# A two-FFN decoder layer on one core: block sums of the Strassen weights moved to GpSimd, with new orders on ScalarE, VectorE and TensorE

## The reference

```python
def _half_ffn(x, norm_g, w_gate, w_up, w_down):
    h = _rmsnorm(x, norm_g)
    return x + 0.5 * ((jax.nn.silu(h @ w_gate) * (h @ w_up)) @ w_down)
# reference(), for the prompt and for the samples
xp = _half_ffn(xp, ffn1_norm, ffn1_w_gate, ffn1_w_up, ffn1_w_down)
u, q, k, v = _project(_rmsnorm(xp, mix_norm), pos_p, w_in, q_norm, k_norm)
mixed = concat([_pool_mix(u, ...), _swa_prompt(q, k, v, attn_sinks)], -1)
xp = xp + mixed @ w_out
xp = _half_ffn(xp, ffn2_norm, ffn2_w_gate, ffn2_w_up, ffn2_w_down)
```

## Time and profile before

| | |
|---|---|
| Median of 3 runs | 915.8 us |
| Lowest to highest | 915.64 to 920.76 us |
| The profiled execution's own time | 918.1 us |
| Its span in the trace | 916.3 us |
| TensorE clock granted, mean | 0.992 of full |
| PE, DVE, ACT, POOL busy | 95%, 75%, 48%, 10% of the span |

### The profile page before, as it was taken

One profiled execution on the slowest core, in us unless ns is written; L12 is line 12 of the kernel. 1 busy time (PEld: TensorE's weight loads), 2 busy tenths in 40 slices (PEclk: granted clock), 3 DMA queues, 4 the chain that ended last, 5 costly groups with the idle time before them and its releaser, 6 DMA issues.

```text
span 916.3 us, 17091 instructions
## 1 busy us (share of the span) xinstructions
PE 867.6 (95%) x6943; PEld 848.0 (93%) x6943; DVE 689.3 (75%) x1046; ACT 436.2 (48%) x702; POOL 89.1 (10%) x84
## 2 busy tenths in 40 slices
PE   9999989998999997999999999998899979999888
PEld 8998989998999997999889999998899979999888
DVE  7976788887888864755885887857888778887744
ACT  8632355545545542434753575423554455554410
POOL 0000011111111100013332001000111111111000
PEclk9999999999999998999999999999999999999989
DMA  8122666686757731422301517227665867677221
GB/s 306 48 82 69 199 158 145 148 199 180 169 122 189 194 83 56 177 84 79 124 25 60 170 61 204 63 70 222 159 152 125 221 171 156 133 197 194 70 93 70
DMA packets 62799, 124.27 MB, mean 136 GB/s; under 512 B 5345, under 2 KB 20833, under 8 KB 62721
## 3 DMA queue, kind: packets, MB, share of 16 engines
q1 hardware_dynamic: 48208, 98.16, 33.6%
q0 software_dynamic: 12784, 22.55, 16.3%
q10 hardware_dynamic: 1728, 2.48, 0.7%
HBM read 119.22 MB, written 3.60 MB: 134 GB/s over the span
## 4 chain that ended last, share of the span: by engine, by line
PE 73%; DVE 14%; issue 5%; DMA 4%; ACT 3%; SPq 1%; DVEq 0%; ACTq 0%
PE ps L757 16%; PE ps L878 14%; PE ps L880 14%; PE ps L879 14%; PE ps L960 10%; DMA full<-gu 4%; DVE wlo L1806 4%; DVE hlo L1927 3%; PE ps L1129 1%; PE ps L1111 1%; ACT whi L1363 1%; DVE hfull L1913 1%; PE ps L1120 1%; DVE gate L1862 1%; ACT u2c L1379 1%
## 5 line engine op out<-in xcount | busy, mean ns | idle before, releaser
L878 PE MATMUL ps<-xhi,whi 128*128 128x260 f32 (+1 forms) x1092 | 313.9, 287 | 35.8 <-ACT u2c L1379 23.2
L879 PE MATMUL ps<-xlo,whi 128*128 128x260 f32 (+1 forms) x1092 | 310.9, 285 | 0.0
L880 PE MATMUL ps<-xhi,wlo 128*128 128x260 f32 (+1 forms) x1092 | 310.5, 284 | 0.0
L878 PEld LDWEIGHTS ps<-xhi,whi 128*128 128x128 f32 x1092 | 205.9, 189 | 41.9 <-issue 28.8
L1806 DVE TENSOR_TENSOR wlo<-full,whi 128x1024 fp32r<-128x1024 f32 (+1 forms) x165 | 210.8, 1305 | 0.0
L880 PEld LDWEIGHTS ps<-xhi,wlo 128*128 128x128 f32 x1092 | 206.5, 189 | 0.0
L879 PEld LDWEIGHTS ps<-xlo,whi 128*128 128x128 f32 x1092 | 206.3, 189 | 0.0
L879 PE MATMUL ps<-hlo,whi 128*128 128x268 f32 (+1 forms) x336 | 95.5, 284 | 0.0
L880 PE MATMUL ps<-hhi,wlo 128*128 128x268 f32 (+1 forms) x336 | 95.4, 284 | 0.0
L878 PE MATMUL ps<-hhi,whi 128*128 128x268 f32 (+1 forms) x336 | 95.4, 284 | 0.0
L2398 POOL DMA_DIRECT2D full<-gu x31 | 37.4, 1207 | 455.2 <-DMA full<-gu 455.2
(11 more groups left out here) (220 smaller groups left out, 1522.8 us busy)
## 6 DMA issues: line engine op xcount, KB each, us to landing
full<-gu SPq DMA_DIRECT2D x78, 512.0 KB, 4.7
full<-gu POOLq DMA_DIRECT2D x31, 512.0 KB, 6.1
full<-d SPq DMA_DIRECT2D x32, 384.0 KB, 3.7
full<-gu SPq DMA_DIRECT2D x39, 256.0 KB, 4.5
full<-d POOLq DMA_DIRECT2D x16, 384.0 KB, 5.3
full<-d SPq DMA_DIRECT2D x8, 768.0 KB, 4.2
raw<-w_in SPq DMA_DIRECT2D x10, 512.0 KB, 3.8
raw<-gu SPq DMA_DIRECT2D x8, 512.0 KB, 3.9
```

The lines of the kernel that those rows point to most:

```text
L878: nc.tensor.matmul(dst, whi_t, mhi_t, start=(first and pr == 0), stop=False, skip_group_check=True)
L879: nc.tensor.matmul(dst, whi_t, mlo_t, start=False, stop=False, skip_group_check=True)
L880: last = nc.tensor.matmul(dst, wlo_t, mhi_t, start=False, stop=(pr == pairs - 1), skip_group_check=True)
```

## The change

1. **Sums.** GpSimd issues no adding transfers any more. It makes all four sums of every Strassen unit itself, 39 x 4 of 128x512 and 16 x 4 of 128x384, in the order block 1 (`s3_made`), 2 (`s2_made`), 5 (`s4_made`), 4 (`s1_made`). VectorE makes none.
2. **Orders.** ScalarE and VectorE cast and split a whole unit ahead: in unit v stand `hi_a`, `hi_b`, `hi_c` of v+1 on ScalarE, with `silu_0` last, and `lo_c` of v, `lo_a` and `lo_b` of v+1 on VectorE. `make_std` moves from the second unit to the first, `pair_sums` ahead of `take_single`, and in whole units the splits go ahead of the other work.
3. **TensorE.** P2 goes ahead of P5. P3 of the last gate unit comes behind two k tiles of the down product, P4 behind three, and in part 3 the last k tiles of the first two output tiles come behind the others of both.
4. **Loads.** Transfer a no longer waits for P2 of the unit three earlier; whole loads and casts wait for P6 instead of P4.

```diff
-                names = [("P1", v), ("P7", v), ("P3", v - 1), ("P6", v), ("P4", v - 1), ("P5", v), ("P2", v)]
+                names = [("P1", v), ("P7", v), ("P3", v - 1), ("P6", v), ("P4", v - 1), ("P2", v), ("P5", v)]
...
             sp.dma_start(full[:, r, 1:5:3, 0:w], src[:, 2:3, :].to_broadcast([P, 2, w])).then_inc(c_loaded[r], 16)
-            if strassen(s, v - 3):
-                sp.wait_ge(products, product_no(s, v - 3, "P2"))
             sp.dma_start(full[:, r, 0:4:3, 0:w], src[:, 0:2, :]).then_inc(a_loaded[r], 16)
...
                     if q == 0:
-                        down(s, v, 0, [0])
+                        down(s, v, 0, [0, 1])
                         p3(s, v - 1)
+                        down(s, v, 0, [2])
                         p4(s, v - 1)
-                        down(s, v, 0, list(range(1, t)))
+                        if unit[1] == 3:
+                            down(s, v, 0, list(range(3, t - 1)))
+                            down(s, v, 1, list(range(t - 1)))
+                            down(s, v, 0, [t - 1])
+                            down(s, v, 1, [t - 1])
+                            continue
+                        down(s, v, 0, list(range(3, t)))
...
+                p2(s, v)
                 p5(s, v)
-                p2(s, v)
...
-                if v:
-                    hi_c(s, v)
-                seed_p1(s, v)
+                if strassen(s, v + 1):
+                    hi_a(s, v + 1)
+                    seed_p1(s, v)
+                    hi_b(s, v + 1)
+                else:
+                    seed_p1(s, v)
+                    d_split_hi(s, v + 1)
                 if pair_to_split(s, v) is not None:
                     pair_hi(s, pair_to_split(s, v))
-                if strassen(s, v + 1):
-                    hi_a(s, v + 1)
                 if u_before and PLAN[s][v - 1][0] == "gate":
                     silu_1(s, v - 1)
                 keep_u2(s, v)
...
                 if strassen(s, v + 1):
-                    hi_b(s, v + 1)
-                else:
-                    d_split_hi(s, v + 1)
-                if unit[0] == "gate":
+                    hi_c(s, v + 1)
+                tiles_hi(s, v)
+                if kind == "gate":
                     silu_0(s, v)
...
     @block.gpsimd
     def _(pool):
-        def add_blocks(s):
...
-                pool.wait_ge(c_loaded[r], 16 * (slot_uses(s, v) + 1))
-                pool.dma_start(full[:, r, 1:5:3, 0:w], src[:, 0:4:3, :], accum_op=ALU.add).then_inc(g_added[r], 16)
+        def weight_sums(s):
...
+                pool.wait_ge(c_loaded[r], k)
+                pool.wait_ge(a_loaded[r], k)
+                add(1, 1, 0).then_inc(s3_made, 1)
+                pool.wait_ge(b_loaded[r], k)
+                pool.wait_ge(s3_made, u + 1)
+                add(2, 1, 6).then_inc(s2_made, 1)
+                pool.wait_ge(s2_made, u + 1)
+                add(5, 2, 3).then_inc(s4_made, 1)
+                add(4, 4, 6).then_inc(s1_made, 1)
```

## The result

| | before | after |
|---|---|---|
| median of 5 | 916.6 us | 926.98 us (924.26 to 928.49) |
| ratio | | 1.0096, 95% interval 1.0061 to 1.013 |
| profiled execution | 918.1, span 916.3 | 925.64, span 923.7 |

The change made the kernel 1% slower. The forecast was 905, a gain.

The account below looks back on a forecast made before the run. TensorE was taken as the bound, busy 867.6 of 916.3 us; waits of 1.2 + 23.0 + 0.3 + 9.3 = 33.8 us against 45.0 gave 11.2 less, 905 us from the median. Range 883 to 928 us, own spread 896 to 914.

Parts of the forecast that it names:

- (a): Gate units 7 to 17: hardly any `u2c` wait, but TensorE waits for `u4c` and `upn`, about 2 us per pair.
- (b): GpSimd adds take 1.3 us alone, 2 to 2.5 when met by VectorE; 1024-element `wlo` averages 1.6 or so, above 1.22.
- (e): VectorE's records come out above 15.9 us per pair of units, by the blocked time.
- (c): The waits of TensorE at the last gate unit are gone.
- (d): Gate units 18 to 21 and the spread units run without waits.
- The pairs: Parts 1 and 2: VectorE sets 23.2 us per pair of units; waits come to 23.0 us, where 19.2 were.
- P2 ahead of P5: Gate units: P5 waits for `u2c` one product later, covering nearly all its waits (23.2 us); `u4c` at P3 is late next.
- P3 and P4 inside the down tile: Last gate units: seven k tiles, 5.2 us, cover the chain to `hlo`; 0.3 of 10.8 us of waits is left.
- At no cost: Loads: transfers a and b land before GpSimd wants them; a load 2 us late would push `hi_a`, `seed_p1` and P6.
- Rival 1: GpSimd's adds slip in beside VectorE for nothing: 34.5 us less, 881 us; chance 0.20.
- Rival 2: VectorE becomes the bound: every add costs it 1.14 us, pairs take 25.0 us in stage 0; 937 us, chance 0.18.
- Rival 3: The wait only moves from P5 to P3, for `u4c`, in half of the units: no change, 916 us; chance 0.20.

Follow-up runs that it names:

- e1_first_units_dve: The changed kernel with the three sums of each stage's first unit made by VectorE as before, the rest on GpSimd: 916.62 us, ratio 0.999.
- e4_pe_order_only: The kernel before with TensorE's new order alone (P2 ahead of P5, P3 and P4 inside the down tile, last k tiles moved): 882.81 us, repeated 881.82.
- e8_p2_before_p5: The kernel before with P2 ahead of P5 in every gate and spread unit, nothing else: 889.2 us, ratio 0.9691.
- e3_write_only: The changed kernel with each GpSimd add replaced by a memset that reads nothing; sums left out, output not the reference's: 864.41 us, ratio 0.9421.
- e13_down_ahead: e4_pe_order_only plus the down weights' cast and split ahead of the last gate unit's work, transfer and cast waiting for P6: 872.02 us, ratio 0.9506.
- e5_orders_only: The changed kernel with all new orders, but sums made as before by the adding transfer and VectorE: 888.62 us, ratio 0.9696.
- e10_orders_mended: e6_seed_first with the places of `make_std`, `pair_sums` and `silu_0` taken back towards the order before: 896.6 us, ratio 0.9772.
- e6_seed_first: e5_orders_only with one exchange on ScalarE, `seed_p1` ahead of the next unit's `hi_a`: 882.47 us, ratio 0.9627.
- e9_write_only_twice: e3_write_only with each memset issued twice, a semaphore wait between the two; sums left out: 869.07 us, ratio 0.9481.

## Why the prediction was wrong

The forecast was 905 us, a gain of 11; measured were 926.98, a loss of 10. The mechanism was right: signs (a), (b) and (e) came out (`u4c` in the place of `u2c`, adds of 1.8 us in the mean, `wlo` at 1.80, VectorE busier by the blocked time). Of (c), the waits for `hlo` went, but 2.4 us of others came at the end of the down tiles; (d) failed, gate units 18 to 21 waited 3.2 us. What failed is the sum, which was made of waits alone, 45.0 before and 33.8 after.

| term of the sum | predicted | measured |
|---|---|---|
| pairs of parts 1 and 2 | 23.0 | 18.9 |
| first gate units behind part 0's down, P1 and P3 | 7.3 | 11.1 |
| second unit of a stage | 1.7 | 3.8 |
| ahead of unit 0: plain products, out-projection | 0 | 5.6 |
| gate units 18 to 21 | 0 | 3.2 |
| last gate unit and end of the down tiles | 0.3 | 2.4 |
| start of the kernel | 1.2 | 1.2 |
| small ones | 0.3 | 0.7 |
| sum | 33.8 | 46.9 |
| clock, excess over before | 0 | 6.1 |

- **The pairs** came out 4.1 us better than forecast, but that is two errors against each other. The pairs of gate units 8 to 11 and 14 to 17 waited 11.5 us, where I had 20.0: 0.59 us per add is blocked, where my 23.2 us per pair had (23.2 - 15.9) / 8 = 0.91. The first pair behind a down part, which I let off with 0.6 and 0.9, waited 3.2 and 3.9 us behind part 1's down product (gate units 12 and 13; the longest waits are 3.00 at 229.29 and 3.33 at 755.76). Why it is late there wasn't looked at.
- **The step that failed** is that the exclusion was followed only where the trace of before had its waits. "In the other gate units VectorE has no pair work ... they run at PE's pace" was a layout for an average unit; they waited 3.2 us in gate units 18 and 19. That the first unit's four adds run beside the token sums of the plain products, and stretch 0.49 us to 1.52, wasn't looked at; e1_first_units_dve shows this place (and its like ahead of stage 1) to be worth 10 us, waits and clock together, as much as the measured loss. Together the terms behind the first line were 17.2 us too low, the first 4.1 too high.
- **The clock** was dropped with "the granted clock is 1.00 in both", read over two windows. Over the whole span, its end left out, the kernel before had 13.65 us at half clock at the waits of the last gate units. They are gone where those waits are shorter (e4_pe_order_only: none). The changed kernel has 27.3 us in other places, which cost 11.9. 12.8 us of waits (forecast 11.2 less, measured 1.6 more) and 6.1 of clock, less 0.2 of starts and ends, make up the 18.7 us between 906.9 and the profiled 925.64.
- **P2 ahead of P5** closed the waits, as said (-25.0 us of waits in e8_p2_before_p5 where I had 19.2). That `u4c` would be late next was no property of this exchange: with the sums where they were it isn't late. I was right that P3 waits in the changed kernel, but the adds are the cause (e3_write_only has all its orders and 0.25 us of waits for `u4c`).
- **P3 and P4 inside the down tile** was worth more than the 10.5 us that I gave it. In e4_pe_order_only, together with the last k tiles' new place, it took the half-clock stretches away (7.4 us in e8_p2_before_p5, 0 here) but left 5.0 us of waits there; the cover also needs the down weights' cast ahead, as the prediction said. e13_down_ahead has both: against e8_p2_before_p5 9.7 us of waits less, 1.0 of starts and ends, 7.4 of clock.
- **At no cost**: transfers were in time with the sums on GpSimd; TensorE nowhere waited for `seed_p1` in the changed kernel. The risk named there, `hi_a` pushing `seed_p1` and P6, is real where the adding transfer stays (e5_orders_only, 15.4 us).
- **Rival 1** (adds free) was given 881 us; e3_write_only, which comes nearest to that case, though its memsets are also shorter than adds, takes 864. The omissions are the same, and the waits fell further than the 34.5 us I gave: 40.5 us of waits less, 6.8 of their starts and ends, 5.8 of clock. **Rival 2** was right on the sign and in part on the mechanism: over the pairs VectorE is busy 91 to 96%, so it nearly is the bound there, but most pairs take 21.6 to 23.3 us and not 25, since an add blocks 0.59 us and not 1.14. At e3_write_only's pace a pair takes 20.7 us in stage 0 and 20.1 in stage 1. The Trainium skill, page "Perfetto Trace Analysis", section "Optimizing Scalar/DVE Operations", warns that moving work between VectorE and GpSimd might not help, as they share a read port. The runs agree, and give the size here: 0.59 us blocked per add against 0.59 saved per sum. **Rival 3** (the wait moves from P5 to P3, 916 us) has the nearest number and tells what the list of waits shows, 21.9 us for `u4c` at P3. But it isn't half of the units, and none of them is a unit without pair work but the first of a stage; and wherever `silu_0` waited, it was for `take_single` on VectorE, not for the cast behind GpSimd's last add.

The prediction also never set the two halves of the change apart. With the sums as before, its own steps gave 916 - 19.2 - 10.5 = 886, near e5_orders_only (888.6) and above e4_pe_order_only; the second half was a loss of 19 us by its own numbers and of 38 by the runs.

## What to carry to other kernels

Before moving two-input work to GpSimd, set the time it blocks VectorE against the time it saves there: here they were equal per sum, and two of a unit's four sums had cost VectorE nothing before, so it lost. The blocking then falls on particular instructions in its chains, the same ones each time: most waits of the changed kernel come back in e1_first_units_dve within 0.1 us. And look at an engine's share stretch by stage: 81% in the mean was 91 to 96% in the pairs. Follow such a lock through every stretch in which the engine now runs, not only through those with waits in the old trace. Cost a change that reorders and a change that moves work apart, since one may carry the other. And count for a wait of TensorE more than the view lists: its start and end (0.25 us here), and a possible stretch at half clock.

## What the runs showed of the hardware

- A listed wait of TensorE costs 0.22 to 0.25 us more than is listed, in all thirteen kernels (9.2 us for 39 waits, 12.9 for 53). Many short waits are dearer than they look: e10_orders_mended.
- Stretches at half clock (0.5 of 2.4 GHz, so 1.2) lasted 3.41 or 6.83 us, the one at the very end of a kernel apart, and cost about 1.5 us per 3.41. In the changed kernel all seven began during or within 1.5 us behind a wait of TensorE of 1.9 to 3.7 us; two others of 2.5 and 3.3 us (127.50, 755.76) had none. Shorter waits had some too: in e6_seed_first a stretch began at 705.50, behind waits of 1.13 and 0.84 us, and in e8_p2_before_p5 one at 334.80, at waits of 1.02 and 1.48. In e10_orders_mended and e13_down_ahead, with no wait over 1.3 us, there was none before the end. So the length of a wait alone doesn't decide. e9_write_only_twice and the repetition of e4_pe_order_only have one in the mixer (423.65, 428.57), whose cause I didn't look for.
- GpSimd's memsets next to VectorE's two-input subtractions kept their 0.96 us for 1024 elements and cost VectorE nothing (1.218 us); copies with one SBUF input cost it 0.12 us each, adds with two 0.59. GpSimd is held up as well: copies of 512 took 0.98 us in the mean instead of 0.61, adds 1.80 instead of 1.30.
